# Sums of squares from two fp32r matmuls instead of one f32 matmul, in a two-block transformer kernel

## What is computed

```python
def rmsnorm(x, g):
    y = xf * lax.rsqrt(jnp.mean(xf * xf, axis=-1, keepdims=True) + RMS_EPS)
    return y * g
# first block, each of 8 heads, over its 128 channels
o = rmsnorm(o, subln_g) * (1.0 - lam_init)
# second block
x = x + memory_cross_attention(rms_norm(x, norm_mem_q[l]), rms_norm(mem, norm_mem_kv[l]), ...)
hf = rms_norm(x, norm_ffn[l])
gate, up = jnp.split(hf @ w_ffn_in[l], 2, axis=-1)
```

## Time and profile before

| what | value |
|---|---|
| median of 3 runs | 1590.91 us |
| the profiled execution | 1590.7 us, span 1588.5 us |
| granted TensorE clock | 0.998 |
| TensorE matmul busy | 1576.0 us (99%) |
| VectorE, ScalarE, GpSimd busy | 57%, 40%, 5% |
| HBM traffic over the span | 95 GB/s |

### The profile page before, as it was taken

The page is one execution under the profiler, slowest core; times in us unless marked ns, Lnnn a source line. Parts: engine busy times, 40 slices in busy tenths (PEclk is TensorE's granted clock), DMA queues, the critical chain, the costliest instruction groups (busy, mean ns, idle before and its releaser), DMA issues.

```text
span 1588.5 us, 18999 instructions
## 1 busy us (share of the span) xinstructions
PE 1576.0 (99%) x7374; PEld 1295.0 (82%) x7374; DVE 911.5 (57%) x1344; ACT 632.8 (40%) x985; POOL 81.8 (5%) x66
## 2 busy tenths in 40 slices
PE   9999999999999999999999999999999999999997
PEld 8877777778888888888887888888888888888886
DVE  7766877656544545357777545555655444434435
ACT  5445666643222222265444334343444322222212
POOL 3000000010000000040000010010002000000002
PEclk9999999999999999999999999999999999999999
DMA  5333232333232323222221232334132333232222
GB/s 202 117 96 102 78 94 73 100 119 100 94 106 93 104 90 98 93 93 96 80 67 60 74 132 87 113 120 146 53 93 93 108 98 99 93 106 93 95 84 74
DMA packets 49673, 155.63 MB, mean 98 GB/s; under 512 B 6192, under 2 KB 9136, under 8 KB 49456
## 3 DMA queue, kind: packets, MB, share of 16 engines
q1 hardware_dynamic: 49136, 153.85, 30.8%
q10 hardware_dynamic: 448, 0.57, 0.1%
HBM read 148.11 MB, written 2.10 MB: 95 GB/s over the span
## 4 chain that ended last, share of the span: by engine, by line
PE 97%; DVE 1%; ACT 1%; DMA 0%; issue 0%; ACTq 0%; DVEq 0%
PE G L935 84%; PE SC L935 4%; PE O L935 2%; PE TP L935 2%; PE M L935 2%; PE TP L1224 1%; PE TP L1271 1%; PE M L1239 0%; DVE X L2327 0%; DMA QK<-T 0%; PE SC L1061 0%; PE TP L1321 0%; ACT L1356 0%; PE M L1155 0%; DVE T L1818 0%
## 5 line engine op out<-in xcount | busy, mean ns | idle before, releaser
L935 PE MATMUL G<-XGh,WH 128*128 128x512 f32 x1248 | 497.2, 398 | 0.0
L935 PE MATMUL G<-XGl,WH 128*128 128x512 f32 x1248 | 486.4, 390 | 0.0
L935 PE MATMUL G<-XGh,WL 128*128 128x512 f32 x1248 | 486.4, 390 | 0.0
L1809 DVE TENSOR_TENSOR WL<-RAW,WH 128x1024 fp32r<-128x1024 f32 (+3 forms) x281 | 339.1, 1207 | 184.7 <-ACT WH L1359 184.1
L1359 ACT ACTIVATE WH<-RAW 128x1024 fp32r<-128x1024 f32 (+3 forms) x281 | 283.7, 1011 | 183.5 <-PE G L935 172.7
L935 PEld LDWEIGHTS G<-XGh,WH 128*128 128x128 f32 x1248 | 234.4, 188 | 57.5 <-issue 7.5
L935 PEld LDWEIGHTS G<-XGh,WL 128*128 128x128 f32 x1248 | 234.2, 188 | 50.0
L935 PEld LDWEIGHTS G<-XGl,WH 128*128 128x128 f32 x1248 | 234.5, 188 | 48.5 <-issue 2.2
L935 PE MATMUL G<-MGh,WH 128*128 128x512 f32 x400 | 156.2, 391 | 0.9 <-ACT T L1687 0.6
L935 PE MATMUL G<-MGl,WH 128*128 128x512 f32 x400 | 155.8, 389 | 0.2 <-DVE MGl L1809 0.2
L935 PE MATMUL G<-MGh,WL 128*128 128x512 f32 x400 | 155.7, 389 | 0.0
(11 more groups left out here) (309 smaller groups left out, 1794.4 us busy)
## 6 DMA issues: line engine op xcount, KB each, us to landing
RAW<-in_up SPq DMA_DIRECT2D x32, 512.0 KB, 3.5
RAW<-in_dn SPq DMA_DIRECT2D x32, 512.0 KB, 3.5
RAW<-in_fg SPq DMA_DIRECT2D x22, 512.0 KB, 3.5
RAW<-in_fu SPq DMA_DIRECT2D x22, 512.0 KB, 3.5
RAW<-in_g SPq DMA_DIRECT2D x16, 512.0 KB, 3.6
RAW<-in_f SPq DMA_DIRECT2D x16, 512.0 KB, 3.5
X<-in_x SPq DMA_DIRECT2D x16, 256.0 KB, 4.2
RAW<-in_q SPq DMA_DIRECT2D x8, 512.0 KB, 3.5
```

What stands on the lines that cost most here:

```text
L935: return e.matmul(dst, st, mv, start=start, stop=stop, skip_group_check=True)
L1809: return e.tensor_tensor(dst, src, hi.bitcast(F32), ALU.subtract)
```

## The change

Seven of the eight heads' sums (all but head 7) and the sums of the norms `mq` and `ffn` are made from two fp32r matmuls: ONE x high half of the squares, then ONE x low half, added in bank M. ONE becomes an fp32r tile; the places that stay float32 use a bitcast of it, ONEF. For the heads, ScalarE writes the high half into MGh[:, h, :] right behind the square (in step sq_a), and a new step sq_lo, a tick later, writes the low half into MGl[:, h, :] on VectorE; ss_a, rs_a and op_a come one tick later than before. Head 7 keeps the old steps. For the two norms, new steps acc_hi (ScalarE) and acc_lo (VectorE) write the halves of the accumulated squares into a free slot of QK; the norm `mq` moves from behind the fourth km projection to behind the fifth, `ffn` keeps its place.

```diff
-CLOSING_A = (("pv_a", 6), ("sq_a", 7), ("ss_a", 8), ("rs_a", 9), ("op_a", 10))
+CLOSING_A = (("pv_a", 6), ("sq_a", 7), ("sq_lo", 8), ("ss_a", 9), ("rs_a", 10), ("op_a", 11))
+CLOSING_LAST = (("pv_a", 6), ("sq_a", 7), ("ss_a", 8), ("rs_a", 9), ("op_a", 10))
...
+                closing = CLOSING_A if h < 7 else CLOSING_LAST
+                for kind, n in closing:
                     self.later(o + n, kind, h)
-                done[h] = self.clock + o + CLOSING_A[-1][1]
+                done[h] = self.clock + o + closing[-1][1]
...
             self.put("km", n)
             if n == 3:
+                self.put("acc_hi", "mq")
+                self.put("acc_lo", "mq")
+            elif n == 4:
                 self.put("norm", "mq")
...
             if f == 0:
+                self.put("acc_hi", "ffn")
+                self.put("acc_lo", "ffn")
                 self.put("norm", "ffn")
...
-        ONE = sb("ONE", [P, P])
+        ONE = sb("ONE", [P, P], F32R)
+        ONEF = ONE[:, :].bitcast(F32)
+        SQh, SQl = QK[:, 0, 7, :], QK[:, 1, 7, :]
...
 # TensorE, norm
+                    if ("acc_hi", arg[0]) in SQH:
+                        e.wait_ge(sq_hi, SQH["acc_hi", arg[0]])
+                        mm(M[:, :], ONE[:, :], SQh, start=True)
+                        e.wait_ge(sq_lo, SQH["acc_hi", arg[0]])
+                        mm(M[:, :], ONE[:, :], SQl, stop=True).then_inc(sum_done, 1)
...
 # TensorE, ss_a
+                    if h < 7:
+                        e.wait_ge(oq_hi, OQH["sq_a", h])
+                        mm(M[:, :], ONE[:, :], MGh[:, h, :], start=True)
+                        e.wait_ge(oq_lo, OQH["sq_a", h])
+                        mm(M[:, :], ONE[:, :], MGl[:, h, :], stop=True).then_inc(ss_done, 1)
...
 # ScalarE, sq_a and acc_hi
+                    if h < 7:
+                        if h == 0:
+                            e.wait_ge(unit_done, unit("va", (1, 3)))
+                        e.wait_ge(o_sq, PVA["pv_a", h])
+                        hi(MGh[:, h, :], head_of(h)).then_inc(oq_hi, 1)
+                elif kind == "acc_hi":
+                    e.wait_ge(acc_done, ACC["sq", arg[0], 7])
+                    hi(SQh, STAT[arg[0]][0]).then_inc(sq_hi, 1)
...
 # ScalarE, rs_a
+                    if arg[0] < 7:
+                        e.wait_ge(oq_lo, OQH["sq_a", arg[0]])
...
 # VectorE, sq_lo and acc_lo
+                elif kind == "sq_lo":
+                    h = arg[0]
+                    e.wait_ge(oq_hi, OQH["sq_a", h])
+                    lo(MGl[:, h, :], head_of(h), MGh[:, h, :]).then_inc(oq_lo, 1)
+                elif kind == "acc_lo":
+                    e.wait_ge(sq_hi, SQH["acc_hi", arg[0]])
+                    lo(SQl, STAT[arg[0]][0], SQh).then_inc(sq_lo, 1)
```

More of the change, by code:

```diff
@@ L297, in attention_a @@
             if i == 3:
-                for kind, n in CLOSING_A:
+                closing = CLOSING_A if h < 7 else CLOSING_LAST
+                for kind, n in closing:
                     self.later(o + n, kind, h)
-                done[h] = self.clock + o + CLOSING_A[-1][1]
+                done[h] = self.clock + o + closing[-1][1]
         return done
@@ L768, in program @@
         ACC = tally("sq", but=[("sq", n, 0) for n in STAT])
+        sq_hi, sq_lo = sem("sq_hi"), sem("sq_lo")
+        SQH = tally("acc_hi")
+        oq_hi, oq_lo = sem("oq_hi"), sem("oq_lo")
+        OQH = tally("sq_a", but=[("sq_a", 7)])
         sum_done, ms_done, r_exp, r_done = sem("sum_done"), sem("ms_done"), sem("r_exp"), sem("r_done")
@@ L1060, in _ @@
                     for _ in range(WARM):
-                        e.matmul(SC[:, 0, 0:P], ONE[:, :], ONE[:, :], start=True, stop=True)
+                        e.matmul(SC[:, 0, 0:P], ONEF, ONEF, start=True, stop=True)
                 elif kind == "v_first":
@@ L1107, in _ @@
                     e.wait_ge(fh_acc, ACCH["sq_half", 6, half])
-                    e.matmul(M[:, hs], ONE[:, :], F[:, 0, hs], start=True, stop=False)
+                    e.matmul(M[:, hs], ONEF, F[:, 0, hs], start=True, stop=False)
                     e.wait_ge(fh_sq, HALF["sq_half", 7, half])
-                    e.matmul(M[:, hs], ONE[:, :], F[:, 2, hs], start=False, stop=True).then_inc(sum_done, 1)
+                    e.matmul(M[:, hs], ONEF, F[:, 2, hs], start=False, stop=True).then_inc(sum_done, 1)
                 elif kind == "vmm":
@@ L1147, in _ @@
                     e.wait_ge(lam_prod, 1)
-                    e.matmul(SC[:, 0, 0:2], ONE[0:HEAD, :], LP, start=True, stop=True).then_inc(lam_sum, 1)
+                    e.matmul(SC[:, 0, 0:2], ONEF[0:HEAD, :], LP, start=True, stop=True).then_inc(lam_sum, 1)
                 elif kind == "norm":
@@ L1153, in _ @@
                         e.wait_ge(*m_free[arg[0]])
-                    e.wait_ge(acc_done, ACC["sq", arg[0], 7])
-                    e.matmul(norm_bank(arg[0])[:, 0:n], ONE[:, :], acc, start=True, stop=True).then_inc(sum_done, 1)
+                    if ("acc_hi", arg[0]) in SQH:
[3 more added lines that the diff above has]
+                        mm(M[:, :], ONE[:, :], SQl, stop=True).then_inc(sum_done, 1)
+                    else:
+                        e.wait_ge(acc_done, ACC["sq", arg[0], 7])
+                        e.matmul(norm_bank(arg[0])[:, 0:n], ONEF, acc, start=True, stop=True).then_inc(sum_done, 1)
                 elif kind == "norm2":
@@ L1159, in _ @@
                     e.wait_ge(acc_done, ACC["sq", "c1", 7])
-                    e.matmul(M[:, :], ONE[:, :], STAT["c1"][0], start=True, stop=True).then_inc(sum_done, 1)
+                    e.matmul(M[:, :], ONEF, STAT["c1"][0], start=True, stop=True).then_inc(sum_done, 1)
                     e.wait_ge(op_done, 8)
                     e.wait_ge(acc_done, ACC["sq", "c2", 7])
-                    e.matmul(O[:, :], ONE[:, :], STAT["c2"][0], start=True, stop=True).then_inc(sum_done, 1)
+                    e.matmul(O[:, :], ONEF, STAT["c2"][0], start=True, stop=True).then_inc(sum_done, 1)
                 elif kind == "cols":
@@ L1236, in _ @@
                 elif kind == "ss_a":
+                    h = arg[0]
                     m_bank(step)
-                    e.wait_ge(o_sq, PVA["pv_a", arg[0]])
-                    e.matmul(M[:, :], ONE[:, :], head_of(arg[0]), start=True, stop=True).then_inc(ss_done, 1)
+                    if h < 7:
[3 more added lines that the diff above has]
+                        mm(M[:, :], ONE[:, :], MGl[:, h, :], stop=True).then_inc(ss_done, 1)
+                    else:
+                        e.wait_ge(o_sq, PVA["pv_a", h])
+                        e.matmul(M[:, :], ONEF, head_of(h), start=True, stop=True).then_inc(ss_done, 1)
                 elif kind == "scores_b":
@@ L1834, in _ @@
                 elif kind == "ones":
-                    e.memset(ONE[:, :], 1.0).then_inc(ones_set, 1)
+                    e.memset(ONEF, 1.0).then_inc(ones_set, 1)
                 elif kind == "xsplit" and arg == (0, 0):
```

## The result

The kernel with the change takes 1588.11 us (median of 16 runs, 1586.49 to 1590.69), the kernel before on the same chip 1591.18 us (16 runs, 1590.17 to 1592.09). The ratio is 0.9982, 95% interval 0.9975 to 0.9989: 3.1 us less. The profiled execution took 1588.53 us with a span of 1586.7, 1.8 less than the span of before.

A forecast was written before the change was run, and what follows sets the result against it. TensorE, busy 99% of the span, bounds the kernel. Six heads and one norm at 0.40 give -2.8, head 1 +0.63, memory norm 0: -2.2 us together, so 1588.7 us; own range 1588.0 to 1589.3, 8-in-10 range 1587.3 to 1590.4.

The forecast's parts named there:

- price of the pair: At each changed sum, two fp32r matmuls hold TensorE 0.46 us against 0.86 for the f32 sum: gain 0.40 a place.
- Head 1: At head 1's sum, near 168 us, TensorE waits 1.03 us for VectorE's low half: net loss 0.63.
- The other six heads: Low halves ready with 1.3 to 3.1 us in hand, head 5 next tightest: no wait, 0.40 gained each.
- The shift of the closing steps: Sum, root and scaling of heads 0 to 6 a tick later: costs nothing by itself.
- The ffn norm: Norm before the feed-forward stage: low half just in time, 0.3 us in hand, 0.40 kept.
- The memory norm: Norm of the memory queries: gain 0 (bounds 0 and 0.40), TensorE's wait growing from 0.3 to 0.7 a gemm later.
- The exclusive lock: At head 3, GpSimd delays the low half to about 221.8 from 220.6; wanted at 222.6, so the sum stays.
- nothing in the attention stage waits for VectorE: Before the change, attention's longest TensorE wait is 0.7 us, on a DMA; none there is for VectorE or ScalarE.
- A: Rival: whole gain, head 1's wait gone if the rotation's DMA lands sooner or VectorE's 2.32 us shrink: 1587.3 to 1587.7; chance 0.20.
- B: Rival: TensorE waits at a second place before 188 us, or the norm at 1221 is late: 1589.3 to 1590.8; chance 0.24.
- C: Rival: VectorE reaches the low half late at every head, seven waits of net +0.63: 1594.9; chance 0.05.
- D: Rival: ONE in the new type is no faster, or the type changes something else: 1590.9; chance 0.03.

The follow-up runs named there:

- waits alone: The change with its halves made and waited for, but the seven heads summed in f32 (both norms keep the pair): 1590.79 us, ratio 0.9999.
- ticks alone: The kernel before with only the closing steps ss_a, rs_a, op_a of heads 0 to 6 a tick later, all f32: 1591.49 us, ratio 1.0000.
- the change again: The same changed kernel, timed and profiled a second time: 1588.27 us, ratio 0.9979 against the kernel before.
- low half never: The change without the heads' low halves; the second matmul takes the high half again, so the output is wrong: 1587.31 us, ratio 0.9974.
- early rotation: The change with the rotation's four input DMAs a tick earlier in SyncE's queue, ahead of a 512 KB weight load: 1587.29 us, ratio 0.9976.
- early rotation, three kernels with the pair: The change with rotation DMAs a tick earlier, 1587.29 us; also `mq` behind the last km projection, 1587.02; also head 7 and `mlp` by the pair, 1586.39.
- early rotation, two with the f32 sum at head 1: Rotation DMAs a tick earlier in the kernel before, 1590.98 us; and in the change with head 1 on f32 sum and old ticks, 1588.26 us.
- the early rotation alone: The kernel before with only the rotation's input DMAs a tick earlier, no pair: 1590.98 us, ratio 1.0002.

## Why the prediction was right, step by step

The forecast was 1588.7 us, measured were 1588.1, inside its own range of 1588.0 to 1589.3 but at its lower edge: 2.2 us of gain were forecast, 3.1 measured. Two terms were sized wrong, both the same way, and so don't cancel: the price of the pair too low, and the mean loss at head 1, as far as the medians say, too high. The measured ratio's interval (1.8 to 4.0 us) holds both numbers.

- **The price of the pair** was sized a little low. I took 0.40 a place, 0.86 less 0.46; every undisturbed place gave 0.45. The pair has its 0.46. The 0.86 is right for the f32 sum itself: in the kernel with the waits alone its two records start 0.43 us apart and the transposes start 0.43 behind the second. What the reading of the earlier trace rows missed stands behind the sum: ten starts of projection matmuls behind it take 2.31 us (138.12 to 140.43), and 2.27 in the change at the same place, where no f32 sum is ahead (137.57 to 139.84). Comparing the same two instructions far apart in both traces takes it in, and gives 0.91. Why the starts are later behind the f32 sum no run shows. Seven places: 0.35 us more than forecast.
- **Head 1** was forecast with a wait of 1.03 us and a net loss of 0.63, at that place, ended by that subtraction. The two profiles of the change show waits of 1.40 and 1.06 (second matmul 1.63 and 1.29 behind the first) and net losses of 0.97 and 0.64. The mechanism holds, but I took the earlier trace rows as fixed. It hangs on a landing that moves. The table has, for each profile, when the rotation's last DMA landed against the start of the second set of transposes of head 2 (a minus is before it), and the stretch round head 1 against before:

| profile | landing | low half in VectorE's queue | stretch |
|---|---|---|---|
| ticks alone | +0.5 | no | +0.47 |
| the change | +0.3 | yes | +0.97 |
| before | 0.0 | no | 0 |
| the change again | -0.1 | yes | +0.64 |
| low half a tick earlier | -0.6 | yes | -0.02 |
| head 1 in f32 | -0.8 | no | -0.10 |
| waits alone (f32 sum) | -0.9 | yes | +0.52 |
| memory norm in f32 | -1.2 | yes | -0.47 |
| low half never | -1.7 | no | -0.55 |
| early rotation, three kernels with the pair | -7.1 | yes | -0.47 to -0.50 |
| early rotation, two with the f32 sum at head 1 | -7.0 to -7.1 | no | -0.10 |

  One rule fits them within 0.1 us, but for the waits alone, where the whole f32 sum stands behind the low half: the stretch ends at the later of TensorE's own pace (14.93 us with the f32 sum, 14.55 with the pair) and the landing plus 15.0 us, or plus 15.7 with the low half in VectorE's queue. Those constants were fitted to these same profiles, so the rule is a description; the early rotation is its test by intervention, and the wait went away. So my 0.63 is near what one execution lost (0.64) and is not the mean: of three profiled executions with this first block two lost 0.64 and 0.97 and one gained 0.47. In the timed runs, eight places would give 3.6 and measured were 3.1, so about half a microsecond is missing, which is the pair's gain at head 1 lost and nearly nothing more. This is worked out, not measured, and the interval of the ratio (1.8 to 4.0 us) leaves room on both sides.
- **The other six heads** had 1.3 to 3.1 us in hand by the forecast, and show no wait. The least in the trace is 0.8, at head 3 (under the lock, below), then 1.2 at head 5. The shift of the closing steps cost nothing, as forecast; the ticks alone show 0.00 at six heads.
- **The ffn norm** came just in time as forecast: in the trace after, the low half ended at 1219.65 and the second matmul was due at 1220.04.
- **The memory norm** gave nothing, as forecast. TensorE's timeline after, against the earlier trace rows:

```profile
1069.19 0.63 PE L949 MATMUL M<-QK,ONE 128*128 128x512 f32 x2
...
1075.27 0.28 PE L949 MATMUL G<-WTh,WL 128*128 128x256 f32 x1
1076.09 0.39 PE L949 MATMUL G<-WTh,WH 128*128 128x256 f32 x1 [0.53 <-DVE QK L1847]
```

  The interval of 0.82 where 0.12 is the pace is a wait of 0.70, where the forecast said 0.7. ScalarE's table load stood at 1069.79, 0.60 behind the sum's start as before, now behind the high half of the gemm ahead (1069.39, 0.38 us).
- **The exclusive lock** of VectorE and GpSimd, which the prediction took from the Trainium skill (SBUF — State Buffer, "SBUF: two separate sides"), did catch the new subtraction, at head 3. GpSimd and VectorE of the change:

```profile
219.57 2.17 POOL L1831 TENSOR_TENSOR T<-T,X 128x512 f32<-128x512 f32 x1 [51.90 <-DVE T L2035]
```

```profile
219.38 1.20 DVE L1847 TENSOR_TENSOR WL<-RAW,WH 128x1024 fp32r<-128x1024 f32 x1
220.51 1.78 DVE L1847 TENSOR_TENSOR MGl<-X,MGh 128x512 fp32r<-128x512 f32 x1
```

  The low half took 1.78 us and not 0.68, and ended 0.55 behind GpSimd's addition (222.29 and 221.74). TensorE wanted it at 223.08, so 0.8 us were in hand, which is what the prediction worked out for the lock (221.8 and 222.6). It takes 1.78 or 1.79 in all nine profiles that have it at this tick, and 0.68 in the one that has it a tick earlier. It moved no time here, but head 3 is the tightest of the six heads, and not head 5. At head 1 the weight subtraction stayed at 2.31 us, and the low half behind it took 0.68.
- **What I did not count**: the start-up. In the other profiles TensorE's first scores start 0.6 us earlier to 1.9 later than in the profile of before, by a wait for a small VectorE product and one for a DMA, with no edit near them. It is as large as head 1's loss, so two spans can't be subtracted to price one edit; the stretches can. The prediction also said that nothing in the attention stage waits for VectorE in the kernel before; the early rotation alone shortens the stretch round head 1 by 0.10, so it did wait there, by less than the view of waits lists.

The rivals: the condition of A, a rotation that lands a microsecond sooner, came true in one of the three profiled executions with the change's first block (that with the memory norm in f32, 1587.3 us), with no edit near it; the early rotation brings it about, with a median 3.6 us below before. So A and the forecast are outcomes of one kernel in different executions, and the median of 1588.1 lies between them. No wait spread to a second place (B) with the sum's own; the kernel with the earlier low half shows what B would be. C and D fell: six of seven heads wait for nothing, and the pair is faster.

## What to carry to other kernels

Where an engine's queue has been waiting on a transfer, its slack downstream is that of the transfer's slowest landing, not that of the one profile: take several profiles, since here three executions showed a loss of 0.97, a loss of 0.64 and a gain of 0.47. Before adding work there, look at what the transfer is queued behind, and move it ahead of the large load. Price an edit in an in-order kernel by the starts of the same instruction in both traces, stretch by stretch, since the start-up alone differed by more than the edit's loss. A wait removed from one instruction of a late queue can come back at a later one (0.27 us at the scores here, in one profile) unless work leaves the queue or the queue starts sooner.

## What the runs showed of the hardware

Four SBUF to SBUF DMAs of 128 KB each, issued 0.4 us behind a 512 KB load, took 4.6 to 6.8 us to land for the last of them, in nine profiles. Issued ahead of that load, 2.2 us behind the one before, they took 2.4 to 2.5 us in the five kernels that put them there. An f32 matmul of 512 columns as two records held TensorE 0.86 us and cost 0.91 with the slower starts behind it, two fp32r ones of the same shape 0.46, at a granted clock of 1.00: the float32 sum costs the time of four fp32r matmuls though the trace shows two records. VectorE's subtraction of 128x1024 took 1.22 us alone, 2.31 where a GpSimd addition had started ahead of it (165.97 against 166.45 in the change), and 1.20 where it started ahead of the addition (219.38 against 219.57); then the addition took 2.17 us where it took 1.70 at head 1.
